# Routing weights of a product-key expert layer: one-hot products on TensorE, or a scatter by DMA into DRAM

## What is computed

```python
q = (xc @ w_q).reshape(T, PEER_HEADS, 2, PEER_QDIM // 2)
s = jnp.einsum('thcd,hcnd->thcn', q, sub_keys, preferred_element_type=f32)
sv, si = lax.top_k(s, PEER_TOPK)
comb = (sv[:, :, 0, :, None] + sv[:, :, 1, None, :]).reshape(T, PEER_HEADS, PEER_TOPK * PEER_TOPK)
cv, ci = lax.top_k(comb, PEER_TOPK)
...
eidx = i1 * PEER_NKEYS + i2
w = jax.nn.softmax(cv, axis=-1)
u = u_tab[eidx]
a = jax.nn.gelu(jnp.einsum('td,thkd->thk', xc, u, preferred_element_type=f32)) * w
return jnp.einsum('thk,thkd->td', a.astype(v_tab.dtype), v_tab[eidx])
```

## Time and profile before

| what | value |
|---|---|
| median of 3 runs | 3023.3 us (3018.91 to 3024.06) |
| span of the profiled execution | 3017.1 us (no whole time of its own is listed; 6.2 us under the median) |
| TensorE busy | 2875.0 us, 95% |
| VectorE busy | 2073.7 us, 69% |
| ScalarE busy | 1501.7 us, 50% |
| GpSimd busy | 60.6 us, 2% |
| mean DMA rate | 172 GB/s |

### The profile page before, as it was taken

How to read it: one execution, slowest core, us unless ns; L and a number is a source line. 1 busy time by engine, 2 the same in 40 slices (tenths; PEclk the granted TensorE clock), 3 DMA queues, 4 the chain that set the end, 5 groups by cost and what they waited for, 6 DMA issues and landing times.

```text
span 3017.1 us, 52823 instructions
## 1 busy us (share of the span) xinstructions
PE 2875.0 (95%) x18004; PEld 2567.0 (85%) x18004; DVE 2073.7 (69%) x3647; ACT 1501.7 (50%) x2607; POOL 60.6 (2%) x118
## 2 busy tenths in 40 slices
PE   8889998899999899999999999999899999999998
PEld 6679787798799799999988888776899999988886
DVE  4567975689765678888965555525588879855555
ACT  2444444544534434448964555114344469845544
POOL 0000100011000000000000000000000000000000
PEclk9999999999999999999999999989999999999999
DMA  5439963499763455553345555540445542355553
GB/s 180 126 113 277 354 224 105 120 301 375 249 180 108 136 175 184 181 181 108 101 155 193 194 191 185 128 126 1 147 157 184 182 157 101 105 188 192 192 193 125
DMA packets 310916, 518.35 MB, mean 172 GB/s; under 512 B 37026, under 2 KB 209442, under 8 KB 310179
## 3 DMA queue, kind: packets, MB, share of 16 engines
q1 hardware_dynamic: 294402, 456.78, 47.7%
q0 software_dynamic: 16416, 60.30, 5.6%
HBM read 515.97 MB, written 1.05 MB: 171 GB/s over the span
## 4 chain that ended last, share of the span: by engine, by line
PE 83%; ACT 7%; DVE 4%; issue 3%; DMA 2%; ACTq 1%; SPq 0%; DVEq 0%
PE ps L915 33%; PE ps L846 11%; PE ps L842 11%; PE ps L843 10%; PE ps L893 3%; ACT spread L1869 1%; DMA tile_ring<-mlp_w_in 1%; ACT spread L1875 1%; PE ps L1282 1%; ACT hot_pair L1869 1%; PE ps L1404 1%; PE ps L817 1%; PE ps L1045 1%; PE ps L776 1%; ACT hot_pair L1875 1%
## 5 line engine op out<-in xcount | busy, mean ns | idle before, releaser
L842 PE MATMUL ps<-x_high,w_high 128*128 128x256 f32 x3264 | 815.9, 287 | 21.6 <-DVE x_low L2570 10.6
L843 PE MATMUL ps<-x_low,w_high 128*128 128x256 f32 x3264 | 804.6, 284 | 0.0
L2070 DVE TENSOR_TENSOR w_low<-tile_ring,w_high 128x1024 fp32r<-128x1024 f32 x360 | 441.1, 1225 | 326.1 <-ACT w_high L1701 325.0
L842 PEld LDWEIGHTS ps<-x_high,w_high 128*128 128x128 f32 x3264 | 628.4, 193 | 29.9 <-issue 15.2
L843 PEld LDWEIGHTS ps<-x_low,w_high 128*128 128x128 f32 x3264 | 629.4, 193 | 0.3
L1701 ACT ACTIVATE w_high<-tile_ring 128x1024 fp32r<-128x1024 f32 x360 | 382.5, 1062 | 473.7 <-PE ps L915 473.7
L846 PE MATMUL ps<-x_high,w_low 128*128 128x256 f32 x3264 | 460.5, 284 | 1.4 <-DVE w_low L2846 1.4
L1849 ACT ACTIVATE w_high<-tile_ring 128x1024 fp32r<-128x1024 f32 x256 | 270.1, 1056 | 314.8 <-PE ps L846 314.3
L846 PEld LDWEIGHTS ps<-x_high,w_low 128*128 128x128 f32 x3264 | 423.7, 193 | 1.6 <-DVE w_low L2846 1.6
L915 PE MATMUL ps<-w_high,x_high 128*128 128x512 f32 x1440 | 387.6, 391 | 21.1 <-DVE x_low L2064 21.1
L915 PE MATMUL ps<-w_high,x_low 128*128 128x512 f32 x1440 | 386.6, 390 | 0.0
(11 more groups left out here) (347 smaller groups left out, 3018.3 us busy)
## 6 DMA issues: line engine op xcount, KB each, us to landing
tile_ring<-peer_u SPq DMA_DIRECT2D x256, 512.0 KB, 3.3
tile_ring<-peer_v SPq DMA_DIRECT2D x256, 512.0 KB, 3.3
arena<-mod_w POOLq DMA_DIRECT2D x112, 512.0 KB, 5.7
tile_ring<-mlp_w_in SPq DMA_DIRECT2D x64, 512.0 KB, 5.1
tile_ring<-mlp_w_out SPq DMA_DIRECT2D x64, 512.0 KB, 5.5
tile_ring<-ret_w_in SPq DMA_DIRECT2D x48, 512.0 KB, 3.9
tile_ring<-peer_w_q SPq DMA_DIRECT2D x32, 512.0 KB, 4.0
tile_ring<-sb_w_qkv SPq DMA_DIRECT2D x24, 512.0 KB, 4.2
```

The lines of the kernel that those rows point to most:

```text
L842: nc.tensor.matmul(dst, cols, x_high[:, c, :], start=c == 0, stop=False)
L843: nc.tensor.matmul(dst, cols, x_low[:, c, :], start=False, stop=False)
L2070: V.tensor_tensor(w_low[:, k % 2, :], tile_ring[:, k, :], w_high[:, k % 2, :].bitcast(F32), ALU.subtract).then_inc(low_ready, 1)
```

## The change

The one-hot products, their operands, the transposes, the memsets and the side buffer are gone. In their place:

- Two DRAM tensors `by_key`, one for each layer, [128 second keys, 128 first keys, 256 tokens] in fp32, 16 MB each. At the start GpSimd clears both with 32 DMAs of 1 MB from an input of zeros, after the first four loads of `mod_w` and ahead of all others, and waits for each.
- VectorE works out for each pick its place in `by_key` (`slot_at`). The exponential and the division are done per token block, at tiles 44 and 84 (`RAISED_AT`).
- GpSimd issues one indirect DMA for each pick number: 128 tokens on 128 partitions, one 4-byte weight each, added to the place in DRAM. That is 128 for each block, 256 for each layer. Ahead of each head of 16 it waits until all earlier ones have landed.
- In the second pass SP waits for the whole scatter behind its first four tiles, then loads four slices of `by_key` at a time (512 KB) into two buffers. VectorE multiplies each slice into `gates`, three tiles ahead (`weigh`).

```diff
+RAISED_AT = (44, 84)
+CLEAR = 8
@@ SP, second pass
-                row_tiles(I["peer_v_2"][l], P)
+                weighed_rows(l)
+            def weighed_rows(l):
+                def spread_group(j, g, begun=True):
+                    if begun or g >= 2:
+                        sp.wait_ge(gate_weighed, j * (2 * RING) + (w0 + RING * (g - 1)))
+                    sp.dma_start(spread_tiles[g % 2][:, :, :],
+                                 by_key[l][:, bass.ds(j * (2 * RING) + RING * g, RING), :]).then_inc(spread_loaded[g % 2], 16)
+                for k in range(RING):
+                    tile(0, k, begun=False)
+                sp.wait_ge(scattered, 16 * TB * P * (l + 1))
+                spread_group(0, 0, begun=False)
+                spread_group(0, 1, begun=False)
@@ GpSimd
             for s in range(RING):
                 load(s, s)
+            n_clear = 0
+            for l in range(DEPTH):
+                for i in range(P // CLEAR):
+                    pool.dma_start(by_key[l][:, i * CLEAR:(i + 1) * CLEAR, :],
+                                   I["zero_rows"].rearrange("p (i t) -> p i t", t=T)).then_inc(cleared, 16)
+                    n_clear += 16
+                    pool.wait_ge(cleared, n_clear)
...
+            landed = 0
+            for l in range(DEPTH):
+                flat = by_key[l].rearrange("a b (t o) -> (a b t) o", o=1)
+                for b in range(TB):
+                    pool.wait_ge(weights_ready, TB * l + b + 1)
+                    for h in range(PEER_H):
+                        if landed:
+                            pool.wait_ge(scattered, landed)
+                        for n in range(h * TOPK, (h + 1) * TOPK):
+                            pool.indirect_dma_start(out=flat, out_offset=bass.IndirectOffsetOnAxis(ap=slot_at[:, b, n:n + 1], axis=0),
+                                                    in_=route[:, b, 2, n:n + 1], in_offset=None,
+                                                    compute_op=ALU.add).then_inc(scattered, 16)
+                            landed += 16
@@ TensorE, first pass
-                with pe.Fori(1, WEIGH_FROM // RING - 1) as j:
+                with pe.Fori(1, P // RING) as j:
                     for k in range(RING):
                         tile(j, k)
...
-                with pe.Fori(0, T // (2 * HOT * RING)) as j:
-                    for k in range(RING):
-                        tile(j, WEIGH_FROM + k)
-                        for b in range(2):
-                            four_tokens(j, 2 * k + b)
@@ ScalarE, first pass
+                for b in range(TB):
+                    with act.Fori(j0, RAISED_AT[b] // RING) as j:
+                        tiles(j)
+                    act.wait_ge(routed, TB * l + b + 1)
+                    A(route[:, b, 2, :], route[:, b, 2, :], ACT.Exp).then_inc(pick_exp, 1)
@@ VectorE
+                def finish(b):
+                    v.wait_ge(pick_exp, TB * l + b + 1)
+                    own = route[:, b, 2, :].rearrange("p (h k) -> p h k", k=TOPK)
+                    ... sum, reciprocal, product: weights_ready
+                    for b in range(TB):
+                        if k == RAISED_AT[b] + 2:
+                            finish(b)
+            def weighed_rows(l):
+                def weigh(k, j):
+                    g = k // RING
+                    if k % RING == 0:
+                        v.wait_ge(spread_loaded[g % 2], j * 16 + 16 * (l * P // (2 * RING) + g // 2 + 1))
+                    own = gates[:, bass.ds(j * (2 * RING) + k, 1), :]
+                    V.tensor_tensor(own, own, spread_tiles[g % 2][:, k % RING, :].unsqueeze(1), ALU.mult).then_inc(gate_weighed, 1)
+                def body(j, ahead=True):
+                    for k in range(2 * RING):
+                        ... w_low, chunk(k + 1), then weigh(k + 3)
```

More of the change, by code:

```diff
@@ L207, in build @@
         eps_rms, eps_ln = const(1), const(1)
+        token_at = [const(1) for _ in range(TB)]
         V_MIX, V_CROSS, V_MEM, V_MLP, V_FINAL = 0, 16, 32, 48, 64
@@ L315, in build @@
         half_f = mem(2, PEER_H * TOPK)
[L317 to L320, removed]
+        by_key = [nc.dram_tensor(f"by_key{l}", (P, P, T), F32).ap() for l in range(DEPTH)]
         const_loaded = sem("const_loaded")
@@ L418, in build @@
         gate_stored = sem("gate_stored")
-        gate_merged = sem("gate_merged")
+        gate_weighed = sem("gate_weighed")
         routed = sem("routed")
         pick_exp = sem("pick_exp")
-        row_hot = sem("row_hot")
-        row_diff = sem("row_diff")
-        act_row_hot = sem("act_row_hot")
+        weight_step = sem("weight_step")
+        weights_ready = sem("weights_ready")
+        cleared = sem("cleared")
+        scattered = sem("scattered")
+        spread_loaded = [sem(f"spread_loaded{s}") for s in range(2)]
         out_ready = sem("out_ready")
@@ L2789, in peer @@
-                while tiles.n < WEIGH_FROM + 1:
-                    tile()
-                    clear()
-                while RING * cleared.n < P - WEIGH_FROM:
-                    clear()
-                rows_of(0, 0)
-                rows_of(0, 1)
-                tile()
-                v.wait_ge(gate_stored, t0 + WEIGH_FROM)
-                n_it = T // (2 * HOT * RING)
-                with v.Fori(0, n_it - 1) as j:
-                    weigh_tiles(j)
-                weigh_tiles(n_it - 1, ahead=False)
@@ L2802, in peer @@
[L2802 to L2807 removed]
+                    V.scalar_tensor_tensor(half_f[:, 0, :], route[:, b, 1, :], float(P), route[:, b, 0, :],
+                                           ALU.mult, ALU.add).then_inc(dve_step, 1)
+                    settle()
+                    V.tensor_scalar(slot_at[:, b, :], half_f[:, 0, :], float(T), token_at[b], ALU.mult, ALU.add)
@@ new lines, in peer @@
+                    V.tensor_tensor(route[:, b, 2, :].rearrange("p (h k) -> p h k", k=TOPK), pick_v,
+                                    pick_v[:, :, 0:1].broadcast_to([P, PEER_H, TOPK]), ALU.subtract).then_inc(routed, 1)
+                    v.wait_ge(routed, TB * l + b + 1)
+                    assert tiles.n <= RAISED_AT[b] + 2
+                t0, last = l * P, RAISED_AT[1] + RING
+                while tiles.n < last:
+                    tile()
+                with v.Fori(last // RING, P // RING) as j:
+                    for k in range(RING):
+                        low(k, j)
```

255 lines of the change are left out of this document (102 added, 153 removed).

## The result

| | before | after |
|---|---|---|
| median | 3023.6 us (3018.91 to 3024.06, 4 runs beside those of after) | 3524.1 us (3521.71 to 3527.89, 4 runs) |
| ratio | | 1.166, 95% interval 1.1645 to 1.1678 |
| span of the profiled execution | 3017.1 us | 3521.7 us |

What follows compares the result with a forecast made beforehand. TensorE, busy 95% of the span, was taken as the bound. Span: 3017.1 - 152.5 (products) + 254 (late scatter) + 6 (clock) + 20 (clearing) = 3144.6; with 6.2 to the median, 3151 us. Range 2872 to 3560, the forecast's own 3023 to 3331.

Steps and rivals of the forecast that it cites:

- The products removed: Both layers' first passes: without the one-hot products every tile keeps 2.88 us, saving 152.5 us together.
- The second pass at no cost: Second pass: the added multiply and by_key loads hide under TensorE's 2.72 us a tile, so nothing is taken.
- The start of the scatter, and the waits for landing: First pass: block 0's weights ready at 1233.6 us; GpSimd's landing waits of 2.4 us per head, 19 us a block.
- One indirect DMA: GpSimd's scatter: issuing one takes 1.25 us, between 0.53 and 2.93, making SP late by 127 us a layer.
- the middle: Indirect DMA issue on GpSimd: 1.25 us, the middle in ratio between bounds of 0.53 and 2.93 us.
- rival 4: Scatter: nothing overlaps, adding in DRAM reads and writes every element, 519 us late a layer, 3935 us; chance 0.08 with beyond.
- Rival 3: Scatter beside first pass: VectorE's two-operand SBUF reads delay GpSimd's index reads, 101 us a layer, 3353 us; chance 0.19 (or t up to 2.2).
- t: Time for GpSimd to issue one indirect DMA in the scatter, taken as 1.25 us; the forecast covers 1.0 to 1.6.
- Rivals 1 and 2: Scatter hidden (2891 us with the clearing's stall, chance 0.14), or late by less than what was removed (2973 us, chance 0.20).
- rival 1: Scatter: issue is cheap, t up to 0.75 us, and hidden; 2871 us, with the clearing's stall 2891; chance 0.14.
- The clearing: Kernel start: GpSimd's 32 clearing DMAs, 7.4 us each, delay a modulation load and stall VectorE and TensorE by 20 us.
- The clock: Second pass start: TensorE starts from rest at half clock for some 5 us, 3 us a layer, 6 us together.

## Why the prediction was right or wrong

- *The products removed, 152.5 us*: right. The kernel without the scatter and most of the table loads is at 2875.7 us, the sum without the scatter and the clearing is 2871. The 14 us of table loads were not in it; I had priced the second exponential as a switch, 0.36 us, and not looked at what comes behind it in the code.
- *The second pass at no cost*: right. It takes 350.0 us in layer 0 and 350.9 in layer 1 against 348.4 before (1544.4 to 1892.8), and the clock at its start accounts for about as much, so nothing is left for the multiply and the loads.
- *The start of the scatter, and the waits for landing*: right. 1233.8 us; 31 us in each layer against 38.
- *One indirect DMA*: this term was mis-sized, at the sentence "I take the middle in ratio, 1.25 us". It is 882.1 / 512 = 1.72 us of GpSimd and 164.8 / 512 = 0.32 us between two, 2.04 us. 256 x (2.04 - 1.25) = 202 us a layer, less 7 for the landings, is 195 of the 555 - 358 = 197 us that were missing. Of the 0.79 us by which one DMA was priced too low, 0.60 are there when it runs alone (1.55 + 0.30 - 1.25), and 0.18 are what VectorE holds it up on average (1.72 - 1.55), 90 us over the 512 DMAs. SP's wait is 316 us a layer instead of 127, and the second pass is late by it one for one, as forecast.
- Why the middle was wrong: I had asked what the chip does for a DMA (issue, landing) and left out what GpSimd does for this kind of one. Adding alone is 0.59 us of GpSimd's time, and I had put adding down to DRAM, in rival 4. The landing, which made up the upper bound, overlaps.
- *Rival 3, VectorE holding GpSimd up*: it is real. Its price was 0.53 us a DMA in block 0 and 0.26 in block 1; measured 0.47 (2.01 - 1.55) beside the pass, and nothing in the gap, where the last 30 DMAs of block 0 and all of block 1 were issued. The true case is t above 1.6 with this rival on top, the upper part of the range, to which I gave little.
- *Rivals 1 and 2*: they needed a t under 1.00. Only the plain DMA, 0.54 us, has it, and there rival 1's number held: 2887 for 2891. That it fits so well is luck: it has 20 us for a clearing that cost nothing, and lacks the 14 us of table loads that it didn't know of.
- *The clearing, 20 us*: nothing. The 32 DMAs of 1 MB went out 6.8 us apart (18.99 to 228.87 us), not 7.4, and the last had landed at 235.3. The modulation load behind it went out at 235.8, the very time by which it was needed. In spite of a DMA share of 0.81, tile 2 of the first pass comes only 1.5 us later (1107.1 against 1105.56 in the earlier trace rows).
- *The clock, 6 us*: right in kind, and somewhat too much. The granted clock is 0.50 from 1792 to 1797 us and 0.95 in the next five, but the pass starts only at 1794.2. Its first eight matmuls take 3.45 us (1794.22 to 1797.67) where before, at a granted clock of 1.00, they take 1.93 (1544.37 to 1546.30). The second passes are 1.6 and 2.5 us longer than before, 4 us together.
- The sign and the range held: 3524 lies under 3560. The forecast's own range, to 3331, didn't.

## What to carry to other kernels

Price an indirect DMA of GpSimd by its count, not its bytes: here about 1.3 us each when it writes, 1.9 when it adds, and up to 2.9 beside VectorE steps with two operands in SBUF; then multiply before asking how it hides. A scatter behind a deadline pays only for as many DMAs as fit ahead of it, and those are free. Where an unknown term decides and is multiplied by 512, the chances should sit on its upper half as soon as more work than the nearest row is known to be in it.

## What the runs showed of the hardware

- Adding in DRAM took time on the issuing GpSimd, 0.59 us of 1.55, beside the landing.
- Two engines can fall in step: a DMA held up by 1.02 us in each tile of 2.88 us, and a smoother first pass made the kernel 32 us slower.
- Writing 16 MB twice ahead of and beside the first stage, at a DMA share of 0.81, cost no time that could be measured: tile 2 of the first pass came at 1105.4 us without it and at 1105.4 to 1107.7 with it.
- A loop of ScalarE entered behind another table's function reloaded tables in every turn: 82 loads of 1.28 us at its two lines, 6 with one turn outside the loop, and 14 us of the whole.
